# The last stage of a hybrid decoder step: all expert rows loaded at once into a dead weight ring, results written in their place

## The reference

```python
h = x + jnp.concatenate([conv_out, rwkv_out], axis=-1) @ w_out
h = h + hier_moe(rmsnorm(h, norm2_g), ...)      # top-1 group of 4, top-2 of its 8 experts
...
y_prompt = rmsnorm(h_p, norm_f_g)
y_sample = rmsnorm(h_s, norm_f_g)
```

## Time and profile before

| | |
|---|---|
| median of 3 runs | 1298.6 us (1297.3 to 1299.18) |
| the profiled execution: time | 1293.94 us |
| the profiled execution: span | 1292.2 us |
| PE, DVE, ACT, POOL busy | 1139.5, 701.3, 327.5, 227.0 us |
| q1, the queue of SP: bytes moved | 152.31 MB |

### The profile page before, as it was taken

How to read it: one execution, slowest core, us unless ns; L and a number is a source line. 1 busy time by engine, 2 the same in 40 slices (tenths; PEclk the granted TensorE clock), 3 DMA queues, 4 the chain that set the end, 5 groups by cost and what they waited for, 6 DMA issues and landing times.

```text
span 1292.2 us, 23873 instructions
## 1 busy us (share of the span) xinstructions
PE 1139.5 (88%) x9224; PEld 648.2 (50%) x9225; DVE 701.3 (54%) x1237; ACT 327.5 (25%) x619; POOL 227.0 (18%) x282
## 2 busy tenths in 40 slices
PE   3999999999999699999999899974799999999910
PEld 3455555555545588888894455543233333333300
DVE  4288899973233678888852232237234434434346
ACT  4100001111212245555551211110123223222221
POOL 5000000000002222233320011001133333223000
PEclk8999999999999799999999999975799999999965
DMA  6411111110000110011142311045499889999556
GB/s 205 108 33 33 33 32 35 39 39 21 1 1 1 15 18 15 16 19 18 18 136 81 122 66 41 34 186 236 166 366 327 314 319 334 414 401 403 211 229 224
DMA packets 97241, 171.41 MB, mean 133 GB/s; under 512 B 44391, under 2 KB 68638, under 8 KB 87871
## 3 DMA queue, kind: packets, MB, share of 16 engines
q1 hardware_dynamic: 89663, 152.31, 33.4%
q0 software_dynamic: 7488, 17.84, 3.9%
HBM read 153.63 MB, written 25.91 MB: 139 GB/s over the span
## 4 chain that ended last, share of the span: by engine, by line
PE 76%; DVE 12%; DMA 6%; issue 3%; ACT 2%; SPq 1%; ACTq 0%; DVEq 0%; POOL 0%; POOLq 0%
PE ps L1447 27%; PE ps L1894 13%; PE ps L1771 10%; PE ps L1924 6%; PE ps L1474 5%; DMA arena<-in_w_exp_up_dram 2%; PE ps L1495 2%; PE ps L1881 2%; DMA arena<-y_rows 1%; DMA arena<-in_x_prompt_dram 1%; DVE arena L2198 1%; PE ps L1799 1%; PE ps L1483 1%; PE ps L1461 1%; DVE arena L2201 1%
## 5 line engine op out<-in xcount | busy, mean ns | idle before, releaser
L1447 PE MATMUL ps<-arena 128*128 128x512 f32 (+1 forms) x1056 | 346.3, 490 | 0.6 <-ACT arena L915 0.6
L1447 PEld LDWEIGHTS ps<-arena 128*128 128x128 f32 x1056 | 175.3, 192 | 172.7 <-issue 172.0
L1894 PE MATMUL ps<-arena 128*64 x416 | 193.3, 609 | 9.4 <-DVE arena L2599 5.9
L1897 PE MATMUL ps<-arena 128*64 128x512 f32 x416 | 193.4, 609 | 0.0
L2024 DVE SCALAR_TENSOR_TENSOR arena<-arena,cw 128x1024 f32<-128x1024 f32 x240 | 168.2, 779 | 0.4
L1771 PE MATMUL ps<-arena 128*128 128x512 f32 (+1 forms) x288 | 128.1, 600 | 0.0
L1894 PEld LDWEIGHTS ps<-arena 128*64 128x64 f32 x416 | 55.6, 140 | 121.9 <-issue 121.9
L1474 PE MATMUL ps<-arena 64*64 64x64 f32 x2960 | 99.5, 219 | 7.2 <-DVE arena L2210 3.9
L1474 PEld LDWEIGHTS ps<-arena 64*64 64x64 f32 x2960 | 92.6, 135 | 12.0 <-issue 5.8
L1924 PE MATMUL ps<-arena 128*64 x208 | 94.8, 598 | 2.4 <-ACT arena L1260 2.4
L1927 PE MATMUL ps<-arena 128*64 128x512 f32 x208 | 94.8, 598 | 0.0
(11 more groups left out here) (329 smaller groups left out, 1492.0 us busy)
## 6 DMA issues: line engine op xcount, KB each, us to landing
arena<-in_w_exp_gate_dram SPq DMA_DIRECT2D x32, 1024.0 KB
arena<-in_w_exp_up_dram SPq DMA_DIRECT2D x32, 1024.0 KB
arena<-in_w_exp_down_dram SPq DMA_DIRECT2D x32, 1024.0 KB, 10.1
arena<-in_w_in_dram SPq DMA_DIRECT2D x22, 512.0 KB, 4.1
arena<-in_x_prompt_dram SPq DMA_DIRECT2D x16, 512.0 KB, 4.0
arena<-y_rows SPq DMA_DIRECT2D x8, 1024.0 KB
arena<-in_w_out_dram SPq DMA_DIRECT2D x2, 2048.0 KB, 9.5
xn_rows<-arena SPq DMA_DIRECT2D x8, 512.0 KB, 2.9
```

Source lines behind the costliest of these rows:

```text
L1447: ins = pe.matmul(pr[:, n0:n1], win[q % 6][:, c, :], xnT[:, c, n0:n1], start=(c == 0), stop=(c == DC - 1))
L1894: pe.matmul(banks(b)[0:HS, :], xgT[b][:, c, 0:HS], wring_gu[:, bass.ds(slot, 1), 0:2, c, :].rearrange("p a w f -> p (a w) f"), start=(c == ...
L1897: ins = pe.matmul(banks(b)[HS:P, :], xgT[b][:, c, HS:P], wgu[b][:, :, c, :], start=(c == 0), stop=(c == DC - 1))
```

## The change

Each of the nine tiles gets its own buffer of 2 x 1024 words per partition for its expert rows. The nine buffers lie one behind the other from `O_XN` on, 18,432 words, inside the region of the weight ring. The result of tile i is written over its first expert row, and the squares over its second. All nine loads are issued first, each with a semaphore of its own, and the nine stores behind them. The waits of SP for `ff_done` and of DVE for `fin_out` go. On POOL, the copy of the row numbers for the last group's scatter is made ahead, into a tensor `s_last`, right behind the last scatter but one.

```diff
--- before.py
+++ after.py
@@ -333,10 +333,10 @@
         g_idx = [sb(f"g_idx{s}", [P, 1], U32) for s in range(2)]
         s_idx = [sb(f"s_idx{s}", [P, 1], U32) for s in range(2)]
 
-        YS = 3
-        yk = [at(O_XN + s * 2 * D, TOPK, D) for s in range(YS)]
-        fin = [at(O_XN + (2 * YS + s) * D, D) for s in range(2)]
-        fin_sq = [at(O_XN + (2 * YS + 2 + s) * D, D) for s in range(2)]
+        yk = [at(O_XN + i * TOPK * D, TOPK, D) for i in range(NT)]
+        fin = [v[:, 0, :] for v in yk]
+        fin_sq = [v[:, 1, :] for v in yk]
+        s_last = sb("s_last", [P, 1], U32)
 
         def banks(b, n=1):
             return ps[:, b:b + n, :].rearrange("p b n -> p (b n)")
@@ -453,8 +453,9 @@
         gu_psum, gs_done, gmul_done, hx_done, ht_psum, ht_done = (sem(n) for n in (
             "gu_psum", "gs_done", "gmul_done", "hx_done", "ht_psum", "ht_done"))
         yd_psum, ye_act, ye_dve = sem("yd_psum"), sem("ye_act"), sem("ye_dve")
-        yk_in = w_loaded[0:YS]
-        yk_0 = [wgu_0[s] + 32 * len(range(s, NE, RW)) for s in range(YS)]
+        yk_in = [*w_loaded, *x_loaded]
+        yk_0 = [wgu_0[s] + 32 * len(range(s, NE, RW)) for s in range(RW)] + [16 * len(range(4, MT, 6))] + [
+            wd_0[s] + 16 * len(range(s, NE, RW)) for s in range(RW)]
         ff_done, fin_done = sem("ff_done"), sem("fin_done")
         fin_out = [sem(f"fin_out{s}") for s in range(2)]
 
@@ -667,16 +668,12 @@
                 r = rows_of(i)
                 sp.wait_ge(fin_done, i + 1)
                 dst = y_prompt[0, i * P:(i + 1) * P, :] if i < NT - 1 else y_sample.rearrange("b t d -> (b t) d")
-                sp.dma_start(dst, fin[i % 2][0:r, :]).then_inc(fin_out[i % 2], 16)
+                sp.dma_start(dst, fin[i][0:r, :]).then_inc(fin_out[i % 2], 16)
 
             for i in range(NT):
                 r = rows_of(i)
-                if i >= YS:
-                    sp.wait_ge(ff_done, i - YS + 1)
-                sp.dma_start(yk[i % YS][0:r, :, :], y_pairs[i * P:i * P + r, :, :]).then_inc(yk_in[i % YS], 16)
-                if i >= YS:
-                    result_out(i - YS)
-            for i in range(NT - YS, NT):
+                sp.dma_start(yk[i][0:r, :, :], y_pairs[i * P:i * P + r, :, :]).then_inc(yk_in[i], 16)
+            for i in range(NT):
                 result_out(i)
             sp.wait_ge(fin_out[0], 16 * ((NT + 1) // 2))
             sp.wait_ge(fin_out[1], 16 * (NT // 2))
@@ -879,12 +876,26 @@
                                         in_=ye[b], in_offset=None, bounds_check=N * TOPK - 1, oob_is_err=False)\
                     .then_inc(ye_out[b], 16)
 
+            def last_scatter(g, b):
+                pool.wait_ge(si_ready, g + 1)
+                pool.wait_ge(ye_act, g + 1)
+                pool.wait_ge(ye_dve, g + 1)
+                pool.sem_inc(pool_past_waits, 1)
+                pool.indirect_dma_start(out=y_rows, out_offset=bass.IndirectOffsetOnAxis(ap=s_last[:, :], axis=0),
+                                        in_=ye[b], in_offset=None, bounds_check=N * TOPK - 1, oob_is_err=False)\
+                    .then_inc(ye_out[b], 16)
+
             def pool_step(turn, b, left):
                 g = 2 * turn + b
                 if left >= 4:
                     pool.wait_ge(xT_psum, 2 * NT + g + 3)
                     gather(g + 4, b)
+                if left == 0:
+                    last_scatter(g, b)
+                    return
                 scatter(g, b)
+                if left == 1:
+                    pool.tensor_copy(s_last[:, :], s_rows[:, bass.ds(g + 1, 1)]).then_inc(si_ready, 1)
 
             for g in range(2):
                 gather(g, g)
@@ -1287,7 +1298,7 @@
                 if i < NT:
                     r = rows_of(i)
                     act.wait_ge(ff_done, i + 1)
-                    act.activation(fin_sq[i % 2][0:r, :], hres[i][0:r, :], ACT.Square, accum_out=stat[0:r, 0, i:i + 1])\
+                    act.activation(fin_sq[i][0:r, :], hres[i][0:r, :], ACT.Square, accum_out=stat[0:r, 0, i:i + 1])\
                         .then_inc(sq_done, 1)
                 if i >= 1:
                     r = rows_of(i - 1)
@@ -2646,9 +2657,9 @@
 
             def combine(i):
                 r = rows_of(i)
-                dve.wait_ge(yk_in[i % YS], yk_0[i % YS] + 16 * (i // YS + 1))
+                dve.wait_ge(yk_in[i], yk_0[i] + 16)
                 for k in range(TOPK):
-                    ins = dve.scalar_tensor_tensor(out=hres[i][0:r, :], in0=yk[i % YS][0:r, k, :],
+                    ins = dve.scalar_tensor_tensor(out=hres[i][0:r, :], in0=yk[i][0:r, k, :],
                                                    scalar=w_k[0:r, k, i:i + 1], in1=hres[i][0:r, :], op0=ALU.mult,
                                                    op1=ALU.add)
                     if k == 0:
@@ -2667,10 +2678,8 @@
                 link(dve.reciprocal(stat[0:r, 3, i:i + 1], stat[0:r, 2, i:i + 1]))
                 if i == 0:
                     dve.wait_ge(tables2_in, 16 * 6)
-                if i >= 2:
-                    dve.wait_ge(fin_out[i % 2], 16 * (i // 2))
                 dve.wait_ge(ff_done, i + 1)
-                dve.scalar_tensor_tensor(out=fin[i % 2][0:r, :], in0=hres[i][0:r, :], scalar=stat[0:r, 3, i:i + 1],
+                dve.scalar_tensor_tensor(out=fin[i][0:r, :], in0=hres[i][0:r, :], scalar=stat[0:r, 3, i:i + 1],
                                          in1=gain_f[0:r, :], op0=ALU.mult, op1=ALU.mult).then_inc(fin_done, 1)
 
             for i in range(NT + 2):
```

## The result

| | before | changed |
|---|---|---|
| median | 1297.3 us (7 runs) | 1288.24 us (7 runs) |
| ratio, 95% interval | | 0.993 [0.9911, 0.9949] |
| the profiled execution's time | 1293.94 us | 1290.41 us |
| its span | 1292.2 us | 1288.7 us |
| from DVE's last copy of the expert stage to the end of the span | 57.8 us | 49.3 us |

The kernel became faster by 9.1 us in the medians. The forecast was 1289.7 us, with a gain of 8.9.

What follows compares the result with a forecast made beforehand. DVE, held by late-issued loads, was taken to bound the last stage; 7.35 + 1.17 + 0.42 = 8.9 us off the 1298.6 us median gave 1289.7 us, with 1286.8 to 1293.8 for 8 times in 10.

Steps and rivals of the forecast that it cites:

- Part 1, all loads at once: Last stage: nine loads issued in a row end DVE's waits, so tile 8 starts 7.35 us earlier.
- The reason for late loads: SP's queue: load i stands behind the output of tile i-4, so late issue, not bandwidth, makes DVE wait.
- Part 2, stores behind loads at no cost: SP's queue: outputs wait behind all loads, three pile up (1.6 MB, 4 to 5 us), at no cost.
- Part 3, the last wait: Ahead of the last scale: DVE's wait for fin_out goes, saving 1.17 us.
- Part 4, the scatter: Last scatter on POOL: copying the indices ahead starts it 0.42 us earlier, 0.84 us after DVE's copy ends.
- The level: Whole kernel: the gain is subtracted from the runs' median, 1298.6 us, not the profiled 1293.94 us.
- side by side: Rival on the nine loads: engines share among them, tile 0 lands 19.3 us late, 1309.0 us; chance 0.03.
- The rate becomes the bound: Rival on last-stage transfers: the mixed rate falls from 316 to 280 GB/s, giving 1295.2 us; chance 0.05.
- One engine lags: Rival on the loads: one of 16 engines lags by 2.35 us, paid once at tiles 1 and 2, 1292.0 us; chance 0.12.

Runs made afterwards that it cites:

- e11_changed_again: The changed kernel run again with no edit; stage 49.09 us, median 1289.6 us, ratio to the kernel before 0.9944.
- e3_turns: Changed kernel, but SP issues load i, then store i-3 with its wait for the scaled tile; stage 57.43 us, median 1294.15 us.
- e5_turns_stores_last: Changed kernel, but loads from 4 on wait for scaled tile i-4 and all nine stores come last; stage 53.49 us, one run 1297.31 us.
- e1_store_waits: Changed kernel with DVE's waits for the store of tile i-2 (fin_out) put back; stage 55.37 us, median 1293.21 us.
- e6_halves: Changed kernel, but loads of tiles 0 to 2 split into two expert rows, each awaited separately; stage 49.11 us, median 1286.91 us.
- e7_scale_off_dve: Changed kernel, but for tiles 0 to 5 ScalarE and POOL do the last scale instead of DVE; stage 52.97 us, median 1291.9 us.

## Why the prediction was right

- **Part 1, all loads at once** (7.35 us): right to the hundredth, and e11_changed_again has the same 29.1 us from tile 0 to tile 8. The steps behind it held too. The interval without a wait, 3.97 us, read from two places of the old trace, is that of all tiles now. The loads kept order: DVE started on tile 0 5.07 us behind its issue with nine loads in flight. They ran at 424 GB/s, and DVE was busy beside them for 15.6 of the 19 us at unchanged durations.
- **The reason for late loads** was half told. The prediction said "late issue, not bandwidth". e3_turns shows that it is the place behind the stores, and that the free buffers alone are worth nothing. But e5_turns_stores_last shows that of the 8 us of waits some 4.7 came from loads that ran beside a store, in the worst cases from the last one or two of 16 increments, and only 3.3 from the late issue alone. Both vanish once the loads go first, so the sum didn't suffer.
- **Part 2, stores behind loads at no cost**: right. Store 0 took 11.9 us, the data of the backlog was through by 1273.5, and the last scale to the end took 4.64 us for 4.62. The working had the backlog a little small: three stores and 4 to 5 us, where four stores moved in about 5.5 us, behind loads whose end was slow. e1_store_waits measures what it costs if DVE waits: 5.2 us for store 0, besides the last wait of part 3.
- **Part 3, the last wait**: 1.13 us for 1.17.
- **Part 4, the scatter**: 0.32 us for 0.42. The mis-sized step is the path from DVE's copy to the scatter. It took 0.94 us from the end of the copy, not 0.84. In the chain of the changed kernel POOL goes through three instructions there, the wait of line 882 and lines 883 and 884. Behind its own copy it had been two, lines 877 and 878, as the wait for `si_ready` needed none of its own. The third costs the 0.09 us.
- **The level**: subtracting from the median of the runs, instead of trusting the profiled execution, was right. The profiled executions moved by 3.5 us, the medians by 9.1, the stage by 8.5. That 9.1 lies so close to the forecast of 8.9 is luck: the interval of the ratio spans 6.6 to 11.5 us. The stage is the sharper test, 8.5 for 8.9. The 1.5 us between 1289.7 and 1288.24 are mostly the level, since the median of the kernel before was now 1297.3 us and not 1298.6.

Of the rivals, "side by side" is excluded by the first wait of 9.3 us. "The rate becomes the bound" did not happen: loads alone run at 424, not 316 GB/s. Only the last 0.7 MB of loads, with the stores behind them, went at 255 GB/s over 2.8 us, and nobody waited for them. "One engine lags" read load 5 rightly, as its sixteen increments show: 2.1 of the 2.35 us of DVE's wait were for the last of them. What didn't hold is that one long queue would keep the lag, since it came only beside stores. Its counterargument, that the first four loads went out back to back, misread the rows: three did, and the fourth followed at 1247.04. The figure of 358 GB/s that part 1 weighed from the Trainium skill (DMA: Bandwidth & Descriptors, Where 436 GB/s comes from) is not borne out here either, with 424 GB/s over 19 us.

## What to carry to other kernels

Look at what stands ahead of a load in the issuing queue's program, not only at what the load waits for. A load behind a store inherits the store's wait, and spare buffers don't help it. Putting all loads first is free only if nothing waits for the stores behind them, so the results need buffers of their own, here the landed inputs' own place. Count a stage from an event next to it: over the whole span this change would have shown 3.5 us in one pair of profiles.

## What the runs showed of the hardware

- A load of 1.05 MB issued right behind a store took 5.65 to 8.1 us from issue to use, and 4.7 to 5.1 us without one, though the store's bytes account for 1.3 us. In the slowest (load 5 before the change) the last of 16 semaphore increments came 2.1 us after the 15th.
- The last 0.7 MB of nine loads, with stores queued behind them, moved at 255 GB/s over 2.8 us at a DMA share of 0.98, after 424 GB/s; the stores then moved at 401.
- Loads with rows of 4 KB ran at 418 GB/s for 2 us and at 338 and 283 in the next four (e6_halves), with rows of 8 KB at 424 over 19 us, all with the engines 0.95 busy or more.
- DVE's two-input operations went from 1.28 to as much as 3.24 us beside POOL's product of the same size, each ending 1.08 to 1.09 us after it (e7_scale_off_dve).
- The work ahead of the last stage, all but the same in all runs, ended over a range of 12 us in the 13 profiled executions, while the stage of the changed kernel took 49.31 and 49.09 us in its two profiles.
